# A two-block float32 transformer on one core: rows of x normalised before they are turned, the first delta head's front among gmlp's groups, loads reordered, and two smaller edits in the stick-breaking and hgrn mixers

## The reference

```python
# block 1, layer 0
hn   = rms_norm(h, ln_mix_e)                       # the first thing done to x
proj = hn @ w_in_e                                 # 1024 -> gmlp u,v | q,k,v,z of 4 delta heads | 8 gate columns
a_out = gmlp_spatial_gate(gelu(a_uv), v_gain, ws, bs)   # 4 groups of 128 channels: layer norm of v, mixed over 128 tokens
b_out = gated_deltanet(b_qkv, b_z, b_beta, b_a, ...)    # conv of 4 taps, silu, l2 norm of q and k, chunked delta rule
h = h + concat([a_out, b_out]) @ w_out_e
# ... mlp, gate, layer 1 (differential attention), mlp, gate
# block 2, layer 0: hgrn
f = lower + (1 - lower) * sigmoid(hf);  o = hgrn2(q, 1 - f, v, log f);  y = norm(o) * silu(hg)
# block 2, layer 1: stick breaking, 16 heads, 4 query blocks
log_beta = log_sigmoid(z);  lom = where(mask, log_beta - z, 0)
later = cumsum(lom, reverse=True) - lom
w = where(mask, exp(log_beta + later), 0);  o = w @ v
```

## Time and profile before

| | us |
|---|---|
| median of 3 runs (lowest to highest) | 2844.25 (2843.33 to 2844.41) |
| the profiled execution | 2842.29 |
| its span | 2840.5 |
| PE busy in it | 2684.6 (95%) |
| chain that ended last: PE, DVE, ACT, issue | 85%, 7%, 5%, 2% |

### The profile page before, as it was taken

One profiled execution on the slowest core, in us unless ns is written; L12 is line 12 of the kernel. 1 busy time (PEld: TensorE's weight loads), 2 busy tenths in 40 slices (PEclk: granted clock), 3 DMA queues, 4 the chain that ended last, 5 costly groups with the idle time before them and its releaser, 6 DMA issues.

```text
span 2840.5 us, 33246 instructions
## 1 busy us (share of the span) xinstructions
PE 2684.6 (95%) x12235; PEld 2123.9 (75%) x12235; DVE 1544.3 (54%) x1773; ACT 804.3 (28%) x1384; POOL 1519.6 (53%) x815
## 2 busy tenths in 40 slices
PE   5889999999999999999998999899999999899998
PEld 3567778888866666888886887788887666688887
DVE  4356557764567666776455477533333767533322
ACT  3344330110234553011022144201112666311101
POOL 3322346766644345676664643466665434366664
PEclk8999999999999999999999999999999999999999
DMA  4211145654321114565432321233332211233332
GB/s 116 54 43 38 38 124 187 195 169 132 89 74 54 58 60 131 188 193 169 133 89 59 100 65 60 63 97 97 94 100 82 60 52 52 60 94 93 102 96 67
DMA packets 423045, 271.93 MB, mean 96 GB/s; under 512 B 9738, under 2 KB 408980, under 8 KB 422932
## 3 DMA queue, kind: packets, MB, share of 16 engines
q1 hardware_dynamic: 404928, 216.03, 26.1%
q10 hardware_dynamic: 18004, 54.32, 5.7%
HBM read 268.22 MB, written 2.10 MB: 95 GB/s over the span
## 4 chain that ended last, share of the span: by engine, by line
PE 85%; DVE 7%; ACT 5%; issue 2%; ACTq 0%; PEld 0%; DVEq 0%; POOL 0%; PEldq 0%; POOLq 0%
PE ps L410 12%; PE ps L412 12%; PE ps L411 12%; PE pair L410 8%; PE pair L412 8%; PE pair L411 8%; PE ps L1695 2%; PE ps L1697 2%; PE ps L1696 2%; PE ps L813 2%; PE ps L815 2%; PE ps L814 2%; PE pair L1306 1%; DVE arena L523 1%; PE pair L992 1%
## 5 line engine op out<-in xcount | busy, mean ns | idle before, releaser
L372 POOL TENSOR_TENSOR w_lo<-w_raw,w_hi 128x1024 fp32r<-128x1024 f32 x404 | 985.5, 2439 | 1283.0 <-PE ps L412 651.7
L366 POOL TENSOR_SCALAR w_hi<-w_raw 128x1024 fp32r<-128x1024 f32 x404 | 546.9, 1354 | 9.6 <-DMA w_raw<-in_w_in_e_dram 9.6
L410 PE MATMUL ps<-x_hi,w_hi 128*128 128x512 f32 x1048 | 433.7, 414 | 36.9 <-DVE x_lo L738 19.9
L412 PE MATMUL ps<-x_hi,w_lo 128*128 128x512 f32 x1048 | 416.1, 397 | 0.0
L411 PE MATMUL ps<-x_lo,w_hi 128*128 128x512 f32 x1048 | 415.9, 397 | 0.0
L902 ACT ACTIVATE tt<-sq 128x512 f32<-128x512 f32 x128 | 81.0, 633 | 1071.8 <-DVE sq L939 550.9
L410 PEld LDWEIGHTS ps<-x_hi,w_hi 128*128 128x128 f32 x1048 | 201.3, 192 | 93.7 <-issue 45.6
L932 DVE TENSOR_TENSOR m_lo<-tt,m_hi 128x512 fp32r<-128x512 f32 x128 | 256.4, 2009 | 0.0
L411 PEld LDWEIGHTS ps<-x_lo,w_hi 128*128 128x128 f32 x1048 | 202.3, 193 | 44.4 <-issue 5.7
L412 PEld LDWEIGHTS ps<-x_hi,w_lo 128*128 128x128 f32 x1048 | 201.3, 192 | 43.8
L410 PE MATMUL pair<-x_hi,w_hi 128*128 128x512 f32 x536 | 209.1, 390 | 0.0
(11 more groups left out here) (390 smaller groups left out, 4416.6 us busy)
## 6 DMA issues: line engine op xcount, KB each, us to landing
w_raw<-in_w_mlp_dram SPq DMA_DIRECT2D x128, 512.0 KB, 4.2
w_raw<-in_mlp_w_dram SPq DMA_DIRECT2D x128, 512.0 KB, 4.0
arena<-in_ada_w_dram ACTq DMA_DIRECT2D x96, 512.0 KB, 4.2
w_raw<-in_w_in_ab_dram SPq DMA_DIRECT2D x28, 512.0 KB, 3.7
w_raw<-in_w_in_e_dram SPq DMA_DIRECT2D x24, 512.0 KB, 4.0
w_raw<-in_w_qkv_o_dram SPq DMA_DIRECT2D x24, 512.0 KB, 3.7
w_raw<-in_w_qkv_dram SPq DMA_DIRECT2D x24, 512.0 KB, 3.7
w_raw<-in_w_ple_gate_dram SPq DMA_DIRECT2D x16, 512.0 KB, 3.8
```

The costliest lines, as they stand in the source:

```text
L366: nc.gpsimd.tensor_scalar(w_hi[:, j, :, :], w_raw[:, j, :, :], 1.0, 1.0, ALU.mult, ALU.mult).then_inc(w_cut_hi, 1)
L372: nc.gpsimd.tensor_tensor(w_lo[:, j, :, :], w_raw[:, j, :, :], w_hi[:, j, :, :].bitcast(F32), ALU.subtract).then_inc(w_ready, 1)
L410: nc.tensor.matmul(bank[:, :], w_hi[:, j, k, :], hi[:, k, :], start=(k == 0), stop=False)
L412: last = nc.tensor.matmul(bank[:, :], w_lo[:, j, k, :], hi[:, k, :], start=False, stop=(k == ND - 1))
```

## The change

1. **Opening.** x stays as rows. ACT takes the sum of squares of each block of 128 tokens (one Square of 128x1024 with an accumulated sum), Ln and Exp give the root for each token, DVE multiplies the rows by it, and PE turns the products (`y_turn`, four transposes a call: calls 0 to 3 ahead of the first dense matmuls, 4 to 7 between them). The gain is applied by ACT and DVE as they read the turned banks. The norm phase goes, its sums and the copies from the turned x with it. x itself is turned later, eight times four transposes (`raw_turn`) in gmlp's groups 0 to 2, with DVE's `raw_copy` into `h`. Setup, norm and gmlp are now one phase.
2. **Loads.** SP issues two blocks of x, the first weight chunk, the other two blocks, three more chunks, and 18 small loads; ACT issues 11 small ones, the gain's first.
3. **Constants.** The turning of tables and mixing matrices, the level masks and small constants move from the opening into gmlp's groups (some into the first mlp).
4. **Gates and the first head's front.** The gates' 24 matmuls stand in gmlp's group 0, their turn and cumulative sum in groups 0 and 1; the sums of decays, the convolution, silu, squares and the sums of squares of the first head stand in group 3, among its q, k, v and z chunks. The 48 dense matmuls of a group are cut 2, 3, 4, 4, 3 (in rows of blocks, three matmuls each) instead of 4, 4, 4, 4, and the split of a group's result into `m_hi` and `m_lo` moves into the next group.
5. **Stick breaking.** The two `barred` matmuls of an item go (64 in all). The scan multiplies by a mask instead of taking a maximum with its own input, and DVE adds `barred` with one more operation and one more wait on itself in each item.
6. **Hgrn.** Banks 0 and 1 are given out in another order: the next head's chunk of v now waits until ACT has read f, not until DVE has read g.

The functions of the delta front (sums of decays, convolution, silu, squares) keep their instructions and get the head as an argument. The core of the diff:

```diff
-            pe.wait_ge(x_load, 16 * NT)
-            for n in range(ND):
-                if n >= 2:
-                    pe.wait_ge(x_copied, n - 1)
-                for b in range(NT):
-                    last = nc.tensor.transpose(ps[2 + n % 2][:, b * P:(b + 1) * P], x_in[:, b, n * P:(n + 1) * P],
-                                               ident[:, :])
-                last.then_inc(x_turned, 1)
...
+            x_rows(0)
+            x_rows(1)
+            gmlp_weight(sp, 0)
+            x_rows(2)
+            x_rows(3)
+            for c in range(1, 4):
+                gmlp_weight(sp, c)
+            load_small(sp, small_loads()[BY_ACT:])
...
+            for b in range(NT):
+                act.wait_ge(x_block[b], 16)
+                nc.scalar.activation(tt[:, 0:2, :].rearrange("p a t -> p (a t)"), x_in[:, b, :], ACT.Square,
+                                     accum_out=squares_sum[:, b:b + 1]).then_inc(*token("sq"))
+                act.wait_ge(*token.at(b, "sq"))
+                nc.scalar.activation(token_ln[:, b:b + 1], squares_sum[:, b:b + 1], ACT.Ln, scale=1.0 / D, bias=eps_col
+                                     ).then_inc(*token("ln"))
+                act.wait_ge(*token.at(b, "ln"))
+                nc.scalar.activation(token_rs[:, b:b + 1], token_ln[:, b:b + 1], ACT.Exp, scale=-0.5
+                                     ).then_inc(*token("rs"))
+            act.wait_ge(gain_ready, 1)
+            for k in range(ND):
+                act.wait_ge(y_turned, k + 1)
+                nc.scalar.activation(x_hi[:, k, :], ps[2 + k % 4][:, :], ACT.Identity, scale=vt[:, k:k + 1]
+                                     ).then_inc(first_hi, 1)
...
+            for b in range(NT):
+                v.wait_ge(*token.at(b, "rs"))
+                for half in range(2):
+                    s = slice(half * T, half * T + T)
+                    nc.vector.tensor_scalar(y[:, b, s], x_in[:, b, s], token_rs[:, b:b + 1], None, ALU.mult
+                                            ).then_inc(y_half[half], 1)
+            for k in range(ND):
+                v.wait_ge(first_hi, k + 1)
+                nc.vector.scalar_tensor_tensor(out=x_lo[:, k, :], in0=ps[2 + k % 4][:, :], scalar=vt[:, k:k + 1],
+                                               in1=x_hi[:, k, :].bitcast(F32), op0=ALU.mult, op1=ALU.subtract
+                                               ).then_inc(first_lo, 1)
...
+            dense_pair(pe, *gmlp_chunks(0), x_hi, x_lo, normed(0), ahead=lambda k: y_turn(pe, k + 4) if k < 4 else None)
             for g in range(4):
+                step = [0]
+
+                def beside(n):
+
+                    for d in range(step[0], step[0] + n):
+                        chunk = gmlp_chunks(g + 1)[d // 8] if g < 3 else (quads["delta"], d // 8)
+                        dense(pe, *chunk, x_hi, x_lo, ks=[d % 8])
+                    step[0] += n
+
                 gm_v = gm_vs[:, g % 2, :]
+                if g == 0:
+                    tables_turned(pe)
+                beside(2)
                 pe.wait_ge(*freed(*gmlp_chunks(g)[1]))
                 nc.tensor.matmul(ps[2][:, :], ones[:, :], gm_v, start=True, stop=True).then_inc(*gmlp_pe("mean"))
-                front(g + 1, 0)
+                if g == 0:
+                    raw_turn(pe, 0)
+                beside(3)
                 pe.wait_ge(*gmlp_act.at(g, "sq"))
                 nc.tensor.matmul(ps[3][:, :], ones[:, :], sq[:, 0, :], start=True, stop=True).then_inc(*gmlp_pe("var"))
-                front(g + 1, 1)
+                if g < 3:
+                    raw_turn(pe, (1, 4, 7)[g])
+                if g == 0:
+                    gates_logits(pe)
+                beside(4)
                 pe.wait_ge(*gmlp_dve.at(g, "vn"))
                 for b in range(NT):
                     last = nc.tensor.transpose(ps[4][:, b * P:(b + 1) * P], gm_xc[:, b * P:(b + 1) * P], ident[:, :])
                 last.then_inc(*gmlp_pe("turn"))
-                front(g + 1, 2)
+                if g < 2:
+                    raw_turn(pe, (2, 5)[g])
+                if g == 1:
+                    gates_cumsum(pe)
+                if g == 3:
+                    delta_rows(pe, 0)
+                beside(4)
                 pe.wait_ge(*gmlp_act.at(g, "nat"))
                 for b in range(NT):
                     last = nc.tensor.matmul(ps[5][:, b * P:(b + 1) * P], gm_nat[:, b, :], gmlp_wt[:, g, :],
                                             start=True, stop=True)
                 last.then_inc(*gmlp_pe("mix"))
-                front(g + 1, 3)
+                if g < 2:
+                    raw_turn(pe, (3, 6)[g])
+                if g == 0:
+                    gates_turn(pe)
+                beside(3)
+                if g == 3:
+                    beside(12)
+                    delta_k_sum(pe, 0)
+                    beside(2)
+                    delta_q_sum(pe, 0)
...
+            delta_decays_first(act, 0)
+            delta_decays_rest(act, 0)
+            high(3)
+            for x in "qkv":
+                delta_silu(act, 0, x)
+            nc.scalar.activation(c_silu, vt[:, col["c_2"]:col["c_2"] + ND], ACT.Silu)
+            exp_and_ln()
+            delta_squared(act, 0, "k")
+            delta_squared(act, 0, "q")
+            delta_k_root(act, 0)
+            delta_q_root(act, 0)
...
-                    last = nc.tensor.matmul(pair[g % 3][:, r, n - P:n], ident_r[:, :], barred[:, :], start=False, stop=True)
+                    last = nc.tensor.matmul(pair[g % 3][:, r, 0:n], st_q[u % 2][half, b * P:(b + 1) * P],
+                                            st_k[u % 2][half, 0:n], start=True, stop=True)
...
-                    last = nc.vector.tensor_tensor_scan(st_sum[:, r, 0:n][:, ::-1], back, back, 0.0, ALU.add, ALU.max)
+                    last = nc.vector.tensor_tensor_scan(st_sum[:, r, 0:n][:, ::-1], back, st_seen[:, T - n:T][:, ::-1], 0.0,
+                                                        ALU.add, ALU.mult)
...
+                nc.vector.tensor_tensor(buf[:, :, n - P:n], buf[:, :, n - P:n],
+                                        barred[:, :].bitcast(F32).unsqueeze(1).to_broadcast([P, 2, P]), ALU.add
+                                        ).then_inc(st_barred, 1)
+                v.wait_ge(st_barred, g + 1)
...
+        def hgrn_bank(u, x):
+            if x == "q":
+                return ps[6]
+            if u == 0:
+                return ps[1 if x == "f" else 0]
+            return ps[(u + 1) % 2 if x == "g" else u % 2]
+
+        def hgrn_bank_free(u, x):
+            if x == "q":
+                return freed(*(hgrn_chunk(u - 1, "q") if u else hgrn_chunk(0, "f")))
+            if x == "v":
+                return freed(*(hgrn_chunk(u, "f") if u else conv_chunk(3, 1)))
+            if x == "g":
+                return freed(*hgrn_chunk(u - 1, "v"))
+            return freed(*(hgrn_chunk(u - 1, "g") if u > 1 else conv_chunk(3, 2)))
```

More of the change, by code:

```diff
@@ L302, in stream @@
         def stream(sp):
-            sp_square(sp, "gmlp", lambda c: dram["w_in_e"][0][:, bass.ds((c % 2) * 512 + (c // 2) * P, P)], 8)
+            for c in range(4, 8):
+                gmlp_weight(sp, c)
             if has("delta"):
@@ L358, in ada_load_one, with gmlp_weight @@
             queue.dma_start(ada_w[:, m % 4, :], src).then_inc(ada_load[m % 4], 16)
-        def sp_square(sp, name, src, count):
-            for c in range(count):
-                weight_chunk(sp, quads[name] + c // 4, c % 4, src(c))
+        def gmlp_weight(sp, c):
+            weight_chunk(sp, quads["gmlp"] + c // 4, c % 4,
+                         dram["w_in_e"][0][:, bass.ds((c % 2) * 512 + (c // 2) * P, P)])
         def cut_hi(q, j):
@@ L414, in dense, with dense_pair @@
                 last.then_inc(mm_done, 1)
-        def dense_pair(pe, first, second, hi, lo, rhs_ready, wide=False, within=None):
+        def dense_pair(pe, first, second, hi, lo, rhs_ready, wide=False, within=None, ahead=None):
             for k in range(ND + 3):
@@ L422, in dense_pair @@
                     dense(pe, *first, hi, lo, rhs_ready, ks=[k], wide=wide)
+                    if ahead is not None:
+                        ahead(k)
                 if k >= 3:
@@ L506, in setup_tensor, with raw_turn, raw_copy @@
             last.then_inc(ws_turned, 1)
+        def raw_turn(pe, r):
+            b, half = divmod(r, 2)
+            if r:
+                pe.wait_ge(raw_copied, r)
+            for n in range(4):
+                last = nc.tensor.transpose(ps[7][:, n * P:(n + 1) * P], x_in[:, b, (4 * half + n) * P:(4 * half + n + 1) * P],
+                                           ident[:, :])
+            last.then_inc(raw_turned, 1)
+        def raw_copy(v, r):
+            b, half = divmod(r, 2)
+            v.wait_ge(raw_turned, r + 1)
+            nc.vector.tensor_copy(h[:, 4 * half:4 * half + 4, b * P:(b + 1) * P], blocks(ps[7][:, :])).then_inc(raw_copied, 1)
         def ada_sum(pe, layer, quarter, part):
```

(44 more changed lines are left out.)

541 lines of the change are left out of this document (285 added, 256 removed).

## The result

The changed kernel takes 2801.46 us (2799.68 to 2806.56 in 4 runs) against 2843.86 for the kernel before in the same runs: 42.4 us less, a ratio of 0.9855 with an interval of 0.9843 to 0.9867. The forecast was 2794 with a range of 2782 to 2812.

What follows compares the result with a forecast made beforehand. PE was taken as the bound, busy 2684.6 of 2840.5 us, with roughly 156 us of standing to win. Terms -42 (up to K), -5.5 (stick breaking) and -2.5 (hgrn) sum to -50: median 2794, range 2782 to 2812.

Steps and rivals of the forecast that it cites:

- Opening, up to M0: From the start to the mean of gmlp's group 0 (M0): forecast at 33.3 instead of 56.82, 23.5 us earlier.
- The loads that were left out: Opening: DMAs given no cost, as SP issues the same x and weights and the small ones are needed only at 31.
- M0 to M3: Gmlp, from the mean of group 0 to that of group 3: 54.6 us against 47.43 before, M3 at 87.8.
- fuller queues: M0 to M3: 2.4 us for waits from raw copies, masks and tables between steps that PE waits for.
- the rival of a crowded gmlp: Gmlp becomes DVE's and ACT's: 16 PE steps each late by 0.9 us, +13, 2807; chance 0.15.
- means more than 18 us apart: Gmlp: sign that would prove the forecast wrong, with steps each late by DVE.
- M3 to K: From group 3's mean to the second run of k products (K): 35 us against 60.4, K at 122.8, 42 earlier.
- Hgrn: Later layer: two waits of 2.0 for the read of g fall away, -2.5 us, bounds -4 and 0.
- Stick breaking: Barred matmuls save 8.7 us, DVE's added operation costs 3 in six items; net -5.5, bounds -9 and +2.
- the rival in which DVE takes over: Stick breaking: new op and wait over 2.05 us make DVE set the pace, -5.5 becomes +10 to +20, 2812; chance 0.12.
- Slower: Stick breaking: each of 64 scans held up by a POOL op of 2.36 us, 2879 to 2909; chance 0.03.
- nothing: First head's front is chained to something taken for free, K within 5 us of 164.65: 2840 or so; chance 0.03.

Runs made afterwards that it cites:

- e5: The changed kernel without DVE's added operation in stick breaking and without the barred matmuls, so that part of the computation is left out: 2794.23 us, ratio 0.9833.
- e7: The changed kernel with all 29 small loads issued by ACT instead of 11: 2808.44 us, ratio 0.9882 to the kernel before.
- e4: The kernel before with only the new hgrn banks: 2844.24 us, ratio 1.0012 to the kernel before.

## Why the forecast was right, and where it was not

**Opening, up to M0: right.** Forecast 23.5, measured 23.07. The path came as worked out: ACT's squares from 6.3, scaled rows at 14.9 (forecast 14.3), first dense matmul 18.25 (17.7). Two sizes behind it were off and nearly cancel, which is luck. ACT ends its four blocks at 12.8, 1.0 earlier than the 13.8 that was forecast, and DVE's pass of 0.5 took 2.05 beside POOL (below). The 1.0 us for a low clock at the first dense matmuls didn't come: the granted clock was 1.00. In its place the first three matmuls and those behind each turn start farther apart than 0.23. The loads that were left out cost nothing.

```profile
18.25:21.25 3.00, 3.00 (x18) 2.54 (x17) 2.18 (x4) 1.71 (x4) 2.85 (x3) 1.00 0.34 96
...
33.75:86.41 52.66, 52.32 (x255) 39.20 (x254) 29.78 (x69) 22.14 (x35) 20.21 (x13) 1.00 0.25 66
86.41:122.58 36.17, 31.24 (x132) 22.84 (x131) 24.00 (x41) 14.91 (x25) 14.46 (x9) 0.95 0.22 58
```

**M0 to M3: right.** Forecast 54.6, measured 52.66. PE's own work was forecast at 52.2 and is 52.3, the second window above. For fuller queues I had put 2.4; the waits named in that stretch are 0.34 in all. So the rival of a crowded gmlp did not show. One of its signs did all the same, means more than 18 us apart: the first two are 21.89 apart (33.75 and 55.64), without a wait between them, since the gates' 24 matmuls and four of the turns stand there. The sign was badly chosen.

**M3 to K: right.** Forecast 35, measured 36.17: the wait ahead of the sum of squares was forecast at 3 and is 3.23, and behind it two sums took 1.81, the size that the earlier trace rows has. What was forecast for the convolution beside the groups, 3, shows as 1.59 at the last variance. PE's own work with the slower matmuls was forecast at 28.8 and is 31.2, so the waits are 1.2 under the forecast and the work 2.4 over it. Over the three stretches the misses are +0.4, -1.9 and +1.2; that they end at 42.07 for a forecast of 42 is in part luck.

**Hgrn: wrong in sign.** "Two waits of 2.0 for the read of g fall away, and PE's next wait is about 1 us later in both": the waits fell away, and 1.2, 0.3 and 1.5 came in each of two heads, 2 us more than before, 3 in the stage's length and some 1.3 up to stick breaking. The step looked only at PE's next wait. It did not follow what an earlier PE releases, POOL's split, and what that does to DVE.

**Stick breaking: right in kind, wrong in size.** -5.5 was the sum of -8.7 and +3 (which is -5.7). Measured -7.4 and +7.1, about 0. PE's part was near, and the operation's own mean, 0.626, is just over the 0.6 that was said. The added operation was priced only in the six items at the end and at 0.5; it also makes PE wait in the periods before them, though DVE has 2.05 to spare in each item by the window. The busy share hid that PE waits for the end of this chain once in each period; where DVE's spare time lies it doesn't say. This is the rival in which DVE takes over, at less than its price and with no threshold at 2.05.

**Slower, and nothing:** no scan grew by a POOL operation.

## What to carry to other kernels

What PE stood still for, or did ahead of its first full stages, was worth its whole length here: 42 of 42 us reached the end. A step that is put on an engine with spare time counts in full if it stands between two engines that wait for each other in turn, and the spare time of a window doesn't say so; leave it out once (a run like `e5`) before it is priced. When a wait is removed, follow also what the freed engine releases: here POOL's operation moved by 0.8 us against DVE's product, from behind it to ahead of it, and that cost more than the wait. And measure a stage on into what follows it before its length is called a gain or a loss: here more than half of the 3 us came back in the 406 us behind it.

## What was not expected of the hardware

DVE's pass over the last block of scaled rows is a TENSOR_SCALAR with one input in SBUF. Its median is 0.486, and the one that started at 12.82, while POOL's split of 12.24 to 14.58 ran, took until 0.3 us after POOL was done:

```profile
12.24 2.34 POOL L391 TENSOR_TENSOR w_lo<-w_raw,w_hi 128x1024 fp32r<-128x1024 f32 x1 [2.76 <-DMA w_raw<-in_w_in_e_dram]
...
12.82 2.05 DVE L647 TENSOR_SCALAR h<-arena,small 128x512 f32<-128x512 f32 x1 [0.72 <-ACT small L528]
```

The same pass took 2.58 and 2.57 beside POOL's splits in `e7`. So it isn't only operations with two SBUF inputs that wait. The other thing is how exactly a stage repeats while the total scatters: the hgrn stage took 149.2 to 149.3 in the four traces with the old banks and the old waits, and 152.3 to 152.4 in seven of the nine with the new banks alone, though one kernel's runs lie up to 12 us apart (`e4`).
